# Expert loop of a mixture-of-experts kernel: ScalarE's copy of the next block's tokens moved ahead of its copy of a finished block's result

## The chip, the cores and the metric

One core of one Trainium2 chip. The metric is the device time of one execution in microseconds; the time before is 1798.47 us, the median of three runs (1798.45 to 1799.83).

## The reference, cut to what matters

The kernel computes one whole layer: a bidirectional mLSTM and Fourier mixer, then a mixture of experts with 64 experts of which each of 1024 tokens takes 8, plus a shared expert. The change touches only the routed experts. Tokens are sorted by expert and padded to blocks of 128 rows, and each block goes through one expert:

```python
def expert_block(args):
    xblk, e = args
    g, u = jnp.split(xblk @ w_expert_gu[e], 2, axis=-1)
    return (jax.nn.silu(g) * u) @ w_expert_down[e]
yb = lax.map(expert_block, (xb, block_e)).reshape(n_rows, d)
routed = jax.ops.segment_sum(yb * row_w[:, None].astype(yb.dtype), row_tok, num_segments=n_tok)
```

The gather is `xb = t[row_tok]`, and the `segment_sum` is a scatter-add of each block's 128 rows of 1024 floats into the rows of their tokens. With the inputs given there are 104 blocks.

## The kernel before, in words

Everything is float32. A matmul operand is split into a high part (rounded to fp32r) and a low part (the remainder), and each product is made of three matmuls: high by high, high by low, low by high. ScalarE (ACT) makes high parts with a copy, VectorE (DVE) makes low parts with a subtraction.

The expert loop works in steps, one for each block b, software-pipelined. Each engine has its own written-out order for a step (the function `step` in each engine's block), and semaphores join them. Two steps, for the two buffer parities p, make one turn of a hardware loop.

**TensorE (PE), step b.** `h_transposes(b-1)` (2 transposes, L1351, which wait for DVE's `h_rows(b-1)`), `x_transposes(b+1)` (8 transposes, L1330, into PSUM banks 0 and 1), `gate_up(b)` (24 matmuls, L1343 to L1345), `down(b-1)` (12 matmuls, L1365 to L1367, into PSUM banks 5 and 6). `gate_up(b)` waits for `m_xb` (both halves of block b's tokens), `down(b-1)` for `m_y` (banks 5 and 6 were read out by `y_evac(b-2)`).

**ScalarE, step b.** `h_high(b-1)` copies the transposed hidden rows; `y_evac(b-2, p)` copies the finished result of block b-2 from PSUM to the buffer yB[p]; `x_high(b+1)` copies the transposed tokens of block b+1 and is the high half; then `w_high` makes the high parts of weight chunks of 1024 columns (an expert has six, four of gate/up and two of down); then `silu(b)` (L911); then two more chunks. Which chunks are due is decided at run time from a table: a step in which the expert before last brings in its down weights and the next step's expert is a new one has four chunks ahead of `silu`, and two after it. Other steps have two chunks or none. All the copies have one line in the profile, L692, since they go through one helper; they are told apart by their tiles (`arena<-psum 128x1024` is `y_evac`, `split_rows<-psum 128x1024` is `x_high`, `split_rows<-psum 128x256` is `h_high`, `split_weights<-raw_weights` is `w_high`).

**VectorE, step b.** `h_low(b-1)` (L1931), `x_low(b+1)` (L1923 and L1927, waits for `x_high`), `w_low` for the same two or four chunks (L1938, one subtraction for each; every one of them waits for its own high part with `hi_split`), `h_rows(b)` (L1945, for which PE waits at the start of the next step), then `w_low` for two more chunks. The wait in `w_low` stands ahead of the addresses that it works out from registers:

```python
for c in chunks:
    dve.wait_ge(S("hi_split"), 6 * e + (c + 1))
    high = cols(wsplit, (1 - par) * (2 * WE) + 1024 * c, 1024).bitcast(F32)
    tt(cols(wsplit, ...), cols(raw, (1 - par) * WE + 1024 * c, 1024), high, ALU.subtract)
```

**GpSimd (POOL).** For block b, in step b+2: it waits for `m_xb` of block b+3, copies an index column (L642), issues the gather of block b+5 (L645), copies another index column (L652), then `add_rows(b)` waits for `m_y` (yB is filled) and for the scatter of block b-1 to have landed, and issues the scatter-add of block b (L656). Scatters are so done one after the other, since two of them may add to one row.

**SyncE (SP).** It loads the raw weights of an expert (2 MB gate/up, 1 MB down) into one of two buffers as `w_low` frees them (`lo_split`), and passes on their arrival to ScalarE by `gu_ready` and `dn_ready` (L518).

`y_evac(b-2, p)` waits for two things: that `down(b-2)` is done, and that the scatter of block b-4, which reads the same buffer yB[p], has landed:

```python
def y_evac(b, p):
    act.wait_ge(S("block_done"), b + 2)
    act.wait_ge(S(f"added{p}"), 8 * (b - p) + 16)
    copy(yB[:, p], psY).then_inc(S("m_y"), 1)
```

Of the kernel before, what the change touches and what calls it, by code (L numbers as in the profile page):

```python
# [105 lines left out]
def build(nc, a, out):  # L106

    ctx = ExitStack()
    with ctx:
# [62 lines left out]
        def bank(i):  # L172
            return psum[:, 512 * i:512 * i + 512]
# [516 lines left out]
        def _(act):  # L690
            def copy(o, i):
                return act.activation(o, i, ACT.Copy)  # L692
# [151 lines left out]
            def w_high(par, chunks):  # L844

                for c in chunks:
                    copy(cols(wsplit, (1 - par) * (2 * WE) + 1024 * c, 1024), cols(raw, (1 - par) * WE + 1024 * c, 1024)).then_inc(S("hi_split"), 1)
# [44 lines left out]
            def x_high(b, p):  # L892

                act.wait_ge(S("m_xt"), b + 1)
                if isinstance(b, int) and b == 1:
                    copy(xTh[p], psY).then_inc(S("m_xh"), 1)
                else:
                    copy(xTh[p], psum[:, 0:1024]).then_inc(S("m_xh"), 1)

            def h_high(b):  # L900
                act.wait_ge(S("m_ht"), b + 1)
                copy(hTh, bank(7)[:, 0:2 * P]).then_inc(S("m_hh"), 1)
# [6 lines that stand above are left out]
            def silu(b, p):  # L909
                act.wait_ge(S("m_gu"), b + 1)  # L910
                act.activation(sg[:, p], bank(3 + p)[:, 0:DE], ACT.Silu).then_inc(S("m_sg"), 1)  # L911
# [8 lines left out]
            def step(b, p, here, following):  # L920

                h_high(b - 1)
                if here is not None:
                    y_evac(b - 2, p)
                x_high(b + 1, 1 - p)
                if here is None:
                    act.wait_ge(S("dn_ready"), 2)
                    w_high(1, range(4, 6))
                else:
                    with act.If_ne(act.to_reg(here[0]), 0):  # L930
                        act.wait_ge(S("dn_ready"), here[1] + 2)
                        act.sem_inc(S("passed"), 1)
                        w_high(1 - (here[1] & 1), range(4, 6))
                first, par1 = following[0], 1 - (following[1] & 1)
                with act.If_ne(act.to_reg(first), 0):
                    act.wait_ge(S("gu_ready"), following[1] + 2)
                    act.sem_inc(S("passed"), 1)
                    w_high(par1, range(2))
                silu(b, p)
                with act.If_ne(act.to_reg(first), 0):  # L940
                    w_high(par1, range(2, 4))

            def word(b):
                return word_of(act, b)

            step(1, 1, None, fields(word(1)))
            act.wait_ge(S("table_ready"), 2)
            for i in range(2):
                act.wait_ge(S(f"acc_out{i}"), 64)
            rest = act.value_load(pairs_rest[0:1, 0:1], min_val=NE // 2 - 1, max_val=MAXB // 2 - 1)  # L950
            with act.Fori(0, rest) as i:
                one, two, three = pair_of(act, i)[0:3]
                step(2 * i + 2, 0, one, two)
                step(2 * i + 3, 1, two, three)
# [1115 lines left out]
```

## Time and profile before

| | us |
|---|---|
| median of three runs | 1798.47 |
| the profiled execution's own time | 1800.7 |
| its span, first to last instruction | 1798.9 |
| PE busy | 1711.2 (95%) |
| VectorE busy | 1146.1 (64%) |
| ScalarE busy | 797.5 (44%) |
| GpSimd busy | 522.0 (29%) |

The profile is one execution seen by the hardware profiler. In a timeline each row is the start of an instruction (or of several alike), how long they took, engine, line, operation and tiles, and in brackets how long the engine was idle just before and what ended the wait. All times are counted from the start of the span. PE is TensorE's matmul side, PEld its weight-load side; the first waits of a step are seen on both. "<-" in a list of waits names what was waited for, then total us, number of waits and the longest.

### The profile page before, as it was taken

To read this page: it belongs to the slowest core of one execution; us is meant where nothing else is said; L and a number is where in the kernel's file an instruction comes from. 1 tells how busy PE (TensorE), PEld (TensorE's weight loads), DVE (VectorE), ACT (ScalarE), POOL (GpSimd) and SP (SyncE) were. 2 spreads that over 40 slices of the span, in tenths; PEclk is the share of its full clock that TensorE was granted. 3 is DMA by queue.
4 is the path that set the end of the run, shared out by engine and by line. 5 is a ranking of instruction groups with operands and counts; after the bars stand their busy time and mean duration, and the time that the engine had idled before them with its cause. 6 is when DMAs were issued, how large, how long until landed. Compare 5 with 4: busy or idle time off the path is not lost.

```text
span 1798.9 us, 32529 instructions
## 1 busy us (share of the span) xinstructions
PE 1711.2 (95%) x7475; PEld 1237.0 (69%) x7476; DVE 1146.1 (64%) x1704; ACT 797.5 (44%) x1094; POOL 522.0 (29%) x569
## 2 busy tenths in 40 slices
PE   6999999998889999899999998999999999999987
PEld 1545454446854477788888777888888887888864
DVE  4783765403877869667538888653767687266646
ACT  0211112122231032466547787553767676265624
POOL 2000000004832320134334344433443343333321
PEclk9999999999999999999999999999999999999999
DMA  9652000011344241768859899866789789588863
GB/s 379 258 231 95 1 0 0 1 37 40 108 148 175 105 164 54 300 201 311 282 108 367 286 343 338 290 172 202 255 289 344 203 297 371 98 286 235 232 209 142
DMA packets 95503, 357.79 MB, mean 199 GB/s; under 512 B 19389, under 2 KB 19550, under 8 KB 86757
## 3 DMA queue, kind: packets, MB, share of 16 engines
q1 hardware_dynamic: 65298, 288.49, 42.0%
q0 software_dynamic: 30160, 68.76, 17.1%
q8 instruction: 23, 0.38, 0.1%
q14 instruction: 18, 0.15, 0.0%
q10 hardware_dynamic: 4, 0.02, 0.0%
HBM read 330.96 MB, written 70.62 MB: 223 GB/s over the span
## 4 chain that ended last, share of the span: by engine, by line
PE 72%; DMA 12%; DVE 6%; issue 3%; ACT 3%; SPq 1%; ACTq 1%; DVEq 1%; POOL 1%; POOLq 0%
PE psum L1343 8%; PE psum L1345 8%; PE psum L1344 8%; PE psum L1069 7%; DMA sum_rows<-arena,idxs 7%; PE psum L1174 5%; PE psum L1078 4%; PE psum L1330 4%; DMA raw_weights<-in_w_gu 4%; PE psum L1367 3%; PE psum L1365 3%; PE psum L1366 3%; PE psum L1016 3%; PE psum L1109 3%; ACT split_weights L692 2%
## 5 line engine op out<-in xcount | busy, mean ns | idle before, releaser
L1938 DVE TENSOR_TENSOR split_weights<-raw_weights,split_weights (+1 forms) x366 | 428.5, 1220 | 46.3 <-ACT split_weights L692 39.1
L692 ACT ACTIVATE split_weights<-raw_weights (+1 forms) x366 | 363.8, 1060 | 35.2 <-issue 23.6
L1343 PE MATMUL psum<-split_weights,split_rows 128*128 (+1 forms) x832 | 335.7, 403 | 2.5 <-DVE split_rows L1927 2.5
L1345 PE MATMUL psum<-split_weights,split_rows 128*128 (+1 forms) x832 | 326.3, 392 | 0.0
L1344 PE MATMUL psum<-split_weights,split_rows 128*128 (+1 forms) x832 | 325.1, 391 | 0.0
L692 ACT ACTIVATE arena<-psum 128x1024 f32<-128x1024 f32 (+6 forms) x187 | 154.5, 831 | 374.6 <-PE psum L1069 107.1
L656 POOL DMA_INDIRECT sum_rows<-arena,idxs x102 | 171.9, 1685 | 231.9 <-DMA sum_rows<-arena,idxs 189.5
L692 ACT ACTIVATE split_rows<-psum 128x256 fp32r<-128x256 f32 (+1 forms) x209 | 148.1, 709 | 136.8 <-PE psum L1351 134.0
L1345 PEld LDWEIGHTS psum<-split_weights,split_rows 128*128 128x128 f32 x832 | 156.9, 189 | 34.8
L1343 PEld LDWEIGHTS psum<-split_weights,split_rows 128*128 128x128 f32 x832 | 157.5, 189 | 31.8 <-DVE split_rows L1927 2.6
L642 POOL COPY idxg<-idxT 128x1 uint32 (+1 forms) x107 | 73.0, 682 | 366.5 <-DVE split_rows L1927 294.6
L1344 PEld LDWEIGHTS psum<-split_weights,split_rows 128*128 128x128 f32 x832 | 157.4, 189 | 30.1
L1365 PE MATMUL psum<-split_weights,split_rows 128*128 x416 | 161.9, 389 | 1.5 <-DVE split_rows L1931 1.5
L1367 PE MATMUL psum<-split_weights,split_rows 128*128 x416 | 162.5, 391 | 0.0
L1366 PE MATMUL psum<-split_weights,split_rows 128*128 x416 | 161.8, 389 | 0.0
L645 POOL DMA_INDIRECT arena<-t_rows,idxg x107 | 123.3, 1152 | 93.7 <-POOL idxg L642 91.5
L1927 DVE TENSOR_TENSOR split_rows<-psum,split_rows 128x1024 fp32r<-128x1024 f32 x104 | 126.3, 1214 | 0.0
L1069 PE MATMUL psum<-arena 128*128 128x512 f32 (+1 forms) x320 | 123.9, 550 | 1.3 <-DVE arena L1543 1.3
L911 ACT ACTIVATE arena<-psum 128x256 f32<-128x256 f32 x104 | 39.8, 383 | 186.8 <-PE psum L1345 186.8
L1931 DVE TENSOR_TENSOR split_rows<-psum,split_rows 128x256 fp32r<-128x256 f32 x104 | 43.7, 420 | 108.7 <-ACT split_rows L692 106.9
L1174 PE MATMUL psum<-arena 128*128 128x512 f32 x256 | 111.1, 592 | 0.8 <-issue 0.8
L1330 PE MATMUL psum<-cst,arena 128*128 128x128 f32 x840 | 111.5, 276 | 0.3 <-ACT arena L692 0.3
(306 smaller groups left out, 2300.6 us busy)
## 6 DMA issues: line engine op xcount, KB each, us to landing
raw_weights<-in_w_gu SPq DMA_DIRECT2D x62, 2048.0 KB, 11.5
raw_weights<-in_w_dn SPq DMA_DIRECT2D x62, 1024.0 KB, 10.3
arena<-in_w_ada SPq DMA_DIRECT2D x12, 2048.0 KB, 8.6
arena<-in_toks SPq DMA_DIRECT2D x18, 512.0 KB, 9.4
arena<-job_rows SPq DMA_DIRECT2D x16, 512.0 KB, 3.8
arena<-in_w_vog SPq DMA_DIRECT2D x1, 4160.0 KB, 14.5
arena<-in_w_qk SPq DMA_DIRECT2D x1, 4096.0 KB, 17.3
arena<-in_w_out SPq DMA_DIRECT2D x2, 2048.0 KB, 9.4
```

Source lines behind the costliest of these rows:

```text
L656: pool.indirect_dma_start(out=y_dram[:, :], out_offset=bass.IndirectOffsetOnAxis(ap=idxs[:, p:p + 1], axis=0), in_=yB[:, p], in_offset=Non ...
L692: return act.activation(o, i, ACT.Copy)
L1069: ins = mm(bank(q % 4)[:, 0:n], wqk[:, k, P * c:P * c + P], uT[:, k, o:o + n], start=(k == 0), stop=(k == 7))
L1174: ins = mm(o, mixT[:, k, P * j:P * j + P], wout[:, k, 512 * h:512 * h + 512], start=(k == 4), stop=(k == 3))
L1330: ins = pe.transpose(bank(5 + k // 4 if isinstance(b, int) and b == 1 else k // 4)[:, P * (k % 4):P * (k % 4) + P], xg[:, p, 0:D][:, k::8] ...
L1343: mm(bank(3 + p), xk, part(par, 0, 512 * k), start=(k == 0), stop=False)
L1344: mm(bank(3 + p), xk, part(par, 1, 512 * k), start=False, stop=False)
L1345: ins = mm(bank(3 + p), xl, part(par, 0, 512 * k), start=False, stop=(k == 7))
L1365: mm(bank(first + h), hk, part(par, 0, o), start=(k == 0), stop=False)
L1366: mm(bank(first + h), hk, part(par, 1, o), start=False, stop=False)
L1367: ins = mm(bank(first + h), hl, part(par, 0, o), start=False, stop=(k == 1))
L1938: tt(cols(wsplit, (1 - par) * (2 * WE) + (WE + 1024 * c), 1024), cols(raw, (1 - par) * WE + 1024 * c, 1024), high, ALU.subtract).then_inc( ...
```

## The change

In ScalarE's step, `x_high(b+1)` is put ahead of `y_evac(b-2)`. Nothing else is changed: the same instructions with the same waits.

```diff
             def step(b, p, here, following):
 
                 h_high(b - 1)
+                x_high(b + 1, 1 - p)
                 if here is not None:
                     y_evac(b - 2, p)
-                x_high(b + 1, 1 - p)
                 if here is None:
                     act.wait_ge(S("dn_ready"), 2)
                     w_high(1, range(4, 6))
```

## Rows read from the trace of the kernel before

**Rows 1.** Windows: us, busy time (count) by engine, PEclk, DMA share, GB/s

```profile
956.00:1123.50 167.50, 155.05 (x745) 127.39 (x744) 137.83 (x157) 129.13 (x156) 66.85 (x65) 0.99 0.93 330
...
1530.00:1740.00 210.00, 210.00 (x1032) 176.76 (x1030) 103.96 (x137) 104.75 (x137) 79.10 (x91) 1.00 0.72 208
```

**Rows 2.** Waits in the expert loop, 745 to 1740 us

```profile
POOL sum_rows L656 <- DMA sum_rows<-arena,idxs: 189.5, 63, 6.0
...
PEld psum L1351 <- DVE arena L1945: 34.4, 43, 3.1
ACT arena L692 <- DMA sum_rows<-arena,idxs: 24.2, 19, 2.7
...
PE psum L1351 <- DVE arena L1945: 20.3, 19, 2.7
ACT split_weights L692 <- SPq L518: 9.7, 6, 2.2
```

**Rows 3.** Waits of PE in the stretch 956 to 1123.5 us

```profile
PE psum L1351 <- DVE arena L1945: 12.4, 10, 2.7
```

**Rows 4.** Timeline of ScalarE, a step with four chunks, scatter landed in time

```profile
957.28 1.02 ACT L692 ACTIVATE arena<-psum 128x1024 f32<-128x1024 f32 x1
958.18 1.03 ACT L692 ACTIVATE split_rows<-psum 128x1024 fp32r<-128x1024 f32 x1
959.09 3.91 ACT L692 ACTIVATE split_weights<-raw_weights  x4
```

**Rows 5.** Timeline of VectorE, the same step

```profile
959.59 1.22 DVE L1927 TENSOR_TENSOR split_rows<-psum,split_rows 128x1024 fp32r<-128x1024 f32 x1
960.80 4.63 DVE L1938 TENSOR_TENSOR split_weights<-raw_weights,split_weights  x4
```

**Rows 6.** Timeline of PE: transposes that begin that step and the next

```profile
956.48 0.48 PE L1351 MATMUL psum<-cst,arena 128*128 128x128 f32 x2
956.80 1.06 PE L1330 MATMUL psum<-cst,arena 128*128 128x128 f32 x8
...
965.92 0.47 PE L1351 MATMUL psum<-cst,arena 128*128 128x128 f32 x2
```

**Rows 7.** Timeline of the loop's first step, which has no result to copy

```profile
750.25 1.06 PE L1330 MATMUL psum<-cst,arena 128*128 128x128 f32 x8
...
751.34 1.03 ACT L692 ACTIVATE split_rows<-psum 128x1024 fp32r<-128x1024 f32 x1 [0.51 <-PE psum L1330]
```

**Rows 8.** Timeline of ScalarE where a chunk's weights came late

```profile
972.49 2.01 ACT L692 ACTIVATE split_weights<-raw_weights  x2 [1.95 <-SPq L518]
```

**Rows 9.** Timeline of VectorE, the low part of that chunk

```profile
974.17 1.23 DVE L1938 TENSOR_TENSOR split_weights<-raw_weights,split_weights  x1 [1.58 <-ACT split_weights L692]
```

**Rows 10.** Timeline of VectorE, a step whose low parts began late

```profile
1458.69 4.63 DVE L1938 TENSOR_TENSOR split_weights<-raw_weights,split_weights  x4
```

**Rows 11.** Timeline of PE: transposes that begin that step and the next

```profile
1453.92 0.39 PE L1351 MATMUL psum<-cst,arena 128*128 128x128 f32 x2
...
1463.77 0.51 PE L1351 MATMUL psum<-cst,arena 128*128 128x128 f32 x2 [0.36 <-DVE arena L1945]
```

**Rows 12.** Timeline of a step whose scatter landed late, and the next transposes

```profile
1114.12 1.03 ACT L692 ACTIVATE arena<-psum 128x1024 f32<-128x1024 f32 x1 [2.70 <-DMA sum_rows<-arena,idxs]
...
1117.66 4.63 DVE L1938 TENSOR_TENSOR split_weights<-raw_weights,split_weights  x4
...
1122.74 0.51 PE L1351 MATMUL psum<-cst,arena 128*128 128x128 f32 x2 [2.67 <-DVE arena L1945]
```

**Rows 13.** Timeline of POOL: the index copy ahead of a gather, two steps

```profile
801.77 0.18 POOL L642 COPY idxg<-idxT 128x1 uint32 x1 [3.58 <-DVE split_rows L1927]
...
960.97 1.10 POOL L642 COPY idxg<-idxT 128x1 uint32 x1 [3.49 <-DVE split_rows L1927]
```

**Rows 14.** Chain that ended last: one of twelve scatters in a row

```profile
1060.37 10.43 DMA sum_rows<-arena,idxs
```

**Rows 15.** Windows around the one fall of TensorE's clock in the busy stretch

```profile
1017.70:1022.20 4.50, 4.50 (x19) 3.69 (x18) 3.40 (x6) 3.93 (x5) 1.60 (x1) 0.62 0.98 372
```

## The prediction, made before the changed kernel ran

> **What bounds the kernel now.** I read the windows of the expert loop first. PE is busy for all of the last 210, but for only 155.05 of 167.5 us between 956 and 1123.5, where the DMA share is 0.93 and the experts change nearly every block [rows 1]. So the loop runs at PE's pace, a little under the 9.44 us from transposes to transposes in [rows 6], except in stretches. The list of waits says what PE waits for: only the two transposes that begin a step, and always for VectorE's `h_rows`; 43 times on the weight-load side (34.4 us), 19 times long enough to be seen on the matmul side (20.3 us) [rows 2]. Those 43 are the steps with four weight chunks ahead of `h_rows`; in 43 - 19 = 24 of them everything is on time and PE only just waits. The 19 others have a cause further back: ScalarE held up in `y_evac` by a scatter that had not landed (19 waits, 24.2 us in all [rows 2]), or in `w_high` by weights (6 waits, 9.7 us [rows 2]). 12.4 of PE's 20.3 us lie in the dense stretch [rows 2, 3].
>
> **What the change removes.** In a late step the copy of the result waited 2.70 us, ran at 1114.12, and all behind it moved: the low parts began at 1117.66, 3.54 us after the start of `y_evac`, and PE idled 2.67 us [rows 12]. Now `x_high` and `x_low` are done by the time the scatter lands. What stays behind the wait is `w_high` and, behind that, the low parts. From the start of `y_evac` the path becomes: one copy, with the next starting 0.90 us later (957.28 to 958.18 [rows 4]), then the first chunk, then its low part. For the last link see below: 1.68 us from the start of a high chunk to the start of the low one. So 2.58 us instead of 3.54: a late four-chunk step is 0.95 us less late.
>
> This is not 0.95 for each. In the dense stretch the chain that ended last is one scatter after another, 10.43 us for one alone [rows 14], without the start of the next, against a step of 9.4; GpSimd waited for the previous scatter 63 times [rows 2]. The landings are paced by the scatters, and PE follows at a fixed distance. Shortening the distance moves PE forward once: **-0.95 us** for the dense stretch. The few late steps elsewhere have two chunks or none and cost PE nothing now.
>
> **What it moves.** `x_high` ran at 958.18, after `y_evac`. It needs the x transposes, which ran from 956.80; in the first step, where there is no result to copy, they began at 750.25 and `x_high` at 751.34, 1.09 us later [rows 7]. So in the step of [rows 4 to 6] `x_high` would begin at 957.89 and `y_evac`, 0.92 behind it, at 958.8, and end at 959.8. `down(b-1)` needs it only after the 24 gate matmuls, which end about two thirds into the step: no cost. `x_low` comes 0.3 us earlier (958.18 against 957.89): no gain by itself, since `gate_up(b+1)` is a step away.
>
> **What it adds.** `w_high` still comes third, but the idle time that ScalarE had after `h_high`, in which `y_evac` was hidden, is now spent waiting for PE's transposes. The first chunk starts not at 959.09 [rows 4] but at about 959.7, 0.6 us later. Now VectorE: today its first low part starts at 960.80, just as `x_low` ends [rows 5], and 1.71 us after the high chunk began. How much of this is slack? Where the weights themselves were late, ScalarE began the chunk at 972.49 and the low part began at 974.17 with VectorE idle for 1.58 us: 1.68 us from start to start [rows 8, 9]. Two copies take 2.01 us and four 3.91 [rows 4, 8], so one takes 1.06, and some 0.6 us pass between the end of the high part and the low part, with the engine idle: the wait stands ahead of the address arithmetic. Today this is hidden behind `x_low`, and there is no slack left (1.71 against 1.68). So the low parts start at 959.7 + 1.68 = 961.4 instead of 960.80, **0.6 us later**, in each four-chunk step.
>
> Is `h_rows` moved by as much? The four low parts run back to back for 4.63 us, the high parts come every 0.96 us (3.91 for four), so only the first matters; `h_rows` follows their end (960.80 + 4.63 = 965.43), and PE's next transposes start 0.49 behind it, at 965.92 [rows 4 to 6]. The trace has a natural experiment: a step in which the low parts began late by an overrun of the step before, 4.77 us after the transposes (1453.92 to 1458.69) where the on-time step has 4.32 (956.48 to 960.80). It took 9.85 us to the next transposes and PE waited 0.36; the on-time step took 9.44 [rows 5, 6, 10, 11]. The 0.45 us came through as 0.41. So an on-time four-chunk step pays 0.55 to 0.6 us; I take 0.6, since the chain is serial. The lower bound of this term is nothing (were the first low part after all to wait only for `x_low`), the upper the full 0.92 us of a copy.
>
> How many pay? Of the 24, some stand just ahead of a step whose weights arrive late (six such waits, 9.7 us [rows 2], several in consecutive steps; I take four steps ahead of them); the load runs on meanwhile, so the pay is taken off the next wait. Two more, by my reading of the steps, lie inside the scatter-paced stretch. 24 - 6 = 18 pay: 18 x 0.6 = **+10.8 us**. Steps with two chunks or none have 1.5 us or more to spare behind the low parts and pay nothing; if the cover were gone they would pay the same 0.6.
>
> **GpSimd and SyncE.** The index copy that starts the gather took 0.18 us in a step where VectorE was idle and 1.10 us in [rows 13]'s second, where the low parts had begun. In the new order `x_low` ends 0.3 us earlier and VectorE is then idle for nearly 1 us, so the copy will run in the gap; gather and scatter are issued up to 1.2 us earlier (0.92 + 0.3). Only where scatters pace the loop is this worth anything, once, at the entry to the dense stretch: between 0 and 1.2, I take **-0.9 us**, three quarters of it. The Trainium skill ("SBUF — State Buffer", Who interferes with whom) says that a VectorE instruction with two SBUF inputs blocks a GpSimd one that reads SBUF for its whole duration; by that rule the hold-up would be one full subtraction and the sum 0.3 us smaller. The copy was held for 0.92 us, not for the 1.2 of a subtraction, and the sum goes by the row. No SP or POOL instruction is passed by the moved one; SP's down load is released by low parts 0.6 us later, against loads used more than a step later: 0.
>
> **Sum.** 10.8 - 0.95 - 0.9 = +9 us. On the profiled execution that is a span of 1798.9 + 9 = 1807.9 and a time of 1800.7 + 9 = 1809.7; this execution stands 2.2 us above the median of the runs, so for the median I forecast 1798.5 + 9 = **1807.5 us**.
>
> **Rivals.**
> - *Rather faster.* The late steps are relieved and the on-time ones pay nothing, because the low part's address work is done before its wait or ScalarE's first chunk is not pushed back. Against it: [rows 8, 9], and that ScalarE cannot begin `x_high` before the transposes end. If then every late step in the dense stretch gave its wait back, the gain would be as much as the 12.4 us of [rows 3]: 1788 us as an end, with 1792 in the middle. It decides if the landing of scatters moves forward with PE, that is if a scatter in this stretch takes less than a step. Chance 0.07.
> - *No difference.* No pay in on-time steps, but landings stay where they are: -0.95 - 0.9, at most -3: 1796.5 us. Or the pay is absorbed by DMA in most steps (in the stretches with share 0.93 the transfers set the pace, and time given to them is not lost): +3. Chance 0.13.
> - *Worse than forecast.* All 24 pay and nothing is absorbed: +14.4. To this comes TensorE's clock: it fell once in the dense stretch, to 0.62 granted over 4.5 us (partly at 1.2 instead of 2.4 GHz) [rows 15]. It cost 0.38 x 4.5 = 1.7 us. More steps with idle time can bring one more fall: 1798.5 + 14.4 + 1.7 = 1814.6 us. The Trainium skill ("TensorE: Matmul & The Clock Gate", Part 1) says that the clock is gated by how busy the array has been lately. By that rule the new idle time counts towards a fall; the trace has one fall in a stretch with ten waits of PE [rows 3, 15], so few of them bring one. Chance 0.12.
>
> **How the numbers follow.** The forecast has 0.68. What a measurement of this kernel can tell from no change is 0.2%, 3.6 us. Slower: 0.68 + 0.12 = 0.80; same 0.13; faster 0.07. The range leaves out the faster case, the gaining part of the no-difference case and the tail of the worst: 1801 to 1813.5. It holds 0.3 to 0.8 us of pay in 18 steps, less the gains (18 x 0.3 - 1.85 = +3.5; 18 x 0.8 - 0.95 = +13.5), and a little at the low end.
>
> **What would show it.** Right: PE's transposes wait for `h_rows` still 43 times or so, but some 35 to 43 of them on the matmul side too, with the total up by 8 to 10 us; VectorE waits for `split_weights` in about 40 more steps, 0.9 us each; on-time four-chunk steps last 10.0 instead of 9.44 us; `y_evac` starts 0.9 after `x_high`; the index copy takes 0.2 us in nearly all steps; late steps begin their low parts 2.6 us after `y_evac` starts. Wrong: low parts that still follow `x_low` without a gap, or late steps that vanish altogether instead of moving.

## The result and the profile after

The changed kernel takes 1809.43 us, the median of four runs (1807.71 to 1811.19), against 1799.06 us for the kernel before in runs beside it: 10.4 us slower, a ratio of 1.0057 with a 95% interval of 1.004 to 1.0075. The forecast was 1807.5 us, 9 us above the 1798.47 of its time before. The profiled execution took 1810.08 us, its span is 1808.2 us, 9.3 us over the 1798.9 of the one before.

The waits of the expert loop after the change, from 745 to 1740 us, answer to [rows 2]:

```profile
POOL sum_rows L656 <- DMA sum_rows<-arena,idxs: 190.2, 62, 6.9
...
DVE split_weights L1938 <- ACT split_weights L692: 89.0, 84, 1.7
...
PEld psum L1351 <- DVE arena L1945: 43.7, 44, 1.9
...
PE psum L1351 <- DVE arena L1945: 25.2, 44, 1.4
...
ACT arena L692 <- DMA sum_rows<-arena,idxs: 5.9, 8, 1.9
ACT split_weights L692 <- SPq L518: 2.5, 3, 0.9
```

Two things are to be seen. The wait that was to be relieved is relieved: ScalarE waits for a landing 8 times and 5.9 us in all, where it was 19 times and 24.2 us (in the dense stretch 2.3 us where it was 12.5), and the longest wait of PE is 1.4 us where it was 2.7 [rows 2]. And the price is paid in every four-chunk step: PE's matmul side now idles in 44 steps where it was 19 (one of each is the loop's first step; the others are four-chunk steps, of which there are 43), and the weight-load side waits 43.7 us where it was 34.4. That these 9.3 us are just what the span has grown by is partly chance: some of the growth lies outside the loop, as shown below. VectorE waits 84 times, 89.0 us, for a high part of a weight chunk, where it was 34 times and 38.3 us.

One on-time four-chunk step shows how. ScalarE, then VectorE, then PE, from timelines of the changed kernel; they answer to [rows 4 to 6]:

```profile
961.98 1.03 ACT L692 ACTIVATE split_rows<-psum 128x1024 fp32r<-128x1024 f32 x1 [0.51 <-PE psum L1330]
962.90 1.02 ACT L692 ACTIVATE arena<-psum 128x1024 f32<-128x1024 f32 x1
963.80 3.90 ACT L692 ACTIVATE split_weights<-raw_weights  x4
```
```profile
963.37 1.22 DVE L1927 TENSOR_TENSOR split_rows<-psum,split_rows 128x1024 fp32r<-128x1024 f32 x1
965.51 4.63 DVE L1938 TENSOR_TENSOR split_weights<-raw_weights,split_weights  x4 [0.92 <-ACT split_weights L692]
```
```profile
960.54 0.51 PE L1351 MATMUL psum<-cst,arena 128*128 128x128 f32 x2 [0.48 <-DVE arena L1945]
...
970.59 0.51 PE L1351 MATMUL psum<-cst,arena 128*128 128x128 f32 x2 [0.46 <-DVE arena L1945]
```

ScalarE is idle for 0.51 us until the transposes are done, `y_evac` comes 0.92 us behind `x_high`, and the first weight chunk 3.26 us after the step's transposes, where it was 2.61 (959.09 - 956.48). The low part starts 1.71 us after the high one, as before, but now VectorE stands idle for 0.92 of them. The step lasts 10.05 us instead of 9.44.

A late four-chunk step of the changed kernel, ScalarE, VectorE and PE, answers to [rows 12]:

```profile
1115.65 1.03 ACT L692 ACTIVATE arena<-psum 128x1024 f32<-128x1024 f32 x1 [0.37 <-DMA sum_rows<-arena,idxs]
1116.57 2.00 ACT L692 ACTIVATE split_weights<-raw_weights  x2
```
```profile
1118.27 2.36 DVE L1938 TENSOR_TENSOR split_weights<-raw_weights,split_weights  x2 [1.41 <-issue]
```
```profile
1112.81 0.50 PE L1351 MATMUL psum<-cst,arena 128*128 128x128 f32 x2 [1.06 <-DVE arena L1945]
...
1123.84 0.50 PE L1351 MATMUL psum<-cst,arena 128*128 128x128 f32 x2 [1.45 <-DVE arena L1945]
```

The low part starts 2.62 us after `y_evac` does, where it was 3.54. PE waits 1.45 us instead of 2.67. The starts of PE's transposes also give the balance along the way. The changed kernel was 4.67 us behind after the first step of the dense stretch (970.59 against 965.92 [rows 6]), but only 1.10 behind at its end (1123.84 against 1122.74 [rows 12]): the stretch gave back 3.6 us on balance, though two of these steps became longer by 0.6 us each. It was 8.51 us behind when the loop ended (1748.24 against 1739.73, both from the timelines of PE). The rest is the tail, whose granted clock was 0.85 over 60 us where it was 0.90.

The windows of the dense stretch, before at [rows 1], say that TensorE's clock did not fall there this time:

```profile
956.00:1123.50 167.50, 157.10 (x754) 128.21 (x753) 140.56 (x159) 133.15 (x159) 63.15 (x66) 1.00 0.94 334
```

### The profile page after: what moved, and what is told of

It reads as the page before. It is cut to its first block, busy times and chain, and to the rows that moved or that the text cites. A ratio compares the mean times of both kernels' runs of the same rounds, so it can differ in the third digit from the quotient of the medians.

```text
span 1808.2 us, 32529 instructions
## 1 busy us (share of the span) xinstructions
PE 1715.7 (95%) x7475; PEld 1236.4 (68%) x7476; DVE 1146.0 (63%) x1704; ACT 803.0 (44%) x1094; POOL 512.9 (28%) x569
## 4 chain that ended last, share of the span: by engine, by line
PE 64%; DMA 9%; DVE 8%; ACT 7%; issue 6%; ACTq 2%; DVEq 2%; SPq 1%; POOL 1%; POOLq 0%
PE psum L1069 7%; DMA sum_rows<-arena,idxs 6%; PE psum L1343 6%; PE psum L1345 6%; PE psum L1344 6%; ACT split_weights L692 5%; PE psum L1174 5%; PE psum L1330 4%; PE psum L1078 4%; PE psum L1016 3%; PE psum L1109 3%; PE psum L1367 2%; PE psum L1365 2%; PE psum L1366 2%; DVE split_weights L1938 2%
## 5 line engine op out<-in xcount | busy, mean ns | idle before, releaser
L645 POOL DMA_INDIRECT arena<-t_rows,idxg x107 | 163.9, 1532 | 93.7 <-POOL idxg L642 91.4
L642 POOL COPY idxg<-idxT 128x1 uint32 (+1 forms) x107 | 26.5, 248 | 376.3 <-DVE split_rows L1927 304.2
L1945 DVE SCALAR_TENSOR_TENSOR arena<-psum,gcol,arena 128x256 f32<-128x256 f32 x104 | 50.0, 481 | 95.3 <-ACT arena L911 92.7
```

## The experiments

**h_static: the changed kernel with constant addresses on VectorE.** The subtraction is written once for each buffer parity, so that no address is worked out behind the wait.

```diff
-                for c in chunks:
-                    dve.wait_ge(S("hi_split"), 6 * e + (c + 1))
-                    ...
+                def run(q):
+                    for c in chunks:
+                        dve.wait_ge(S("hi_split"), 6 * e + (c + 1))
+                        ...
+                with dve.If_ne(dve.to_reg(par), 0):
+                    run(1)
+                with dve.If_ne(dve.to_reg(par), 1):
+                    run(0)
```

> The changed kernel, with VectorE's weight subtraction written once for each buffer parity inside a branch, so that its addresses are constants and nothing stands between its wait and the subtraction. Theory (the 0.6 us of address arithmetic behind the wait, uncovered by the new order, is what an on-time four-chunk step pays): the low part follows the high part by under 0.1 us instead of 0.6, on-time four-chunk steps go back from 10.05 to about 9.43 us, PE's waits on the matmul side fall from 44 to under 20, and the time is 1793 to 1798 us, below both kernels. Rival (ScalarE's later start itself is the cost, address work or not, or VectorE and GpSimd collide): steps stay near 10 us and the time near 1809.

Measured: 1793.83 us (ten runs), against 1799.42 for the kernel before: ratio 0.9974 (0.9965 to 0.9983). Against the changed kernel's 1809.43 this is 15.6 us less, for the same order and the same work. The on-time step, ScalarE, VectorE and PE:

```profile
817.39 3.90 ACT L692 ACTIVATE split_weights<-raw_weights  x4
```
```profile
818.49 4.70 DVE L1939 TENSOR_TENSOR split_weights<-raw_weights,split_weights 128x1024 fp32r<-128x1024 f32 x4 [0.21 <-ACT split_weights L692]
```
```profile
814.14 0.50 PE L1351 MATMUL psum<-cst,arena 128*128 128x128 f32 x2
...
823.64 0.51 PE L1351 MATMUL psum<-cst,arena 128*128 128x128 f32 x2
```

From start of the high part to start of the low part it is 1.10 us instead of 1.71: the 0.6 us between the two engines are gone, VectorE idles 0.21 instead of 0.92, and the step lasts 9.50 us. On-time four-chunk steps of this kernel last 9.3 to 9.7 us, 9.47 on average, so a tenth of a microsecond is still paid. ScalarE starts its chunks exactly as late as in the changed kernel (3.25 us into the step against 3.26), so its lateness alone costs little. The matmul side waits for `h_rows` 16 times, 12.3 us.

**b_static: the same constant addresses in the kernel before.** The diff is that of h_static on the old order.

> The kernel before with the same constant addresses. Theory: in the old order the arithmetic is hidden behind x_low in every on-time step, so only the steps in which weights arrive late gain, 0.6 us in each of five or six: 1795.5 to 1799 us, and on-time four-chunk steps stay at 9.43. Rival (the arithmetic costs in both orders): all 43 steps shorter, 1790 or less. Second rival (the added branches cost more than they save): above 1801.

Measured: 1797.95 us, ratio 0.9995 (0.9986 to 1.0005), so no difference that can be told. The theory's range holds it; the saving in late-weight steps is not resolved. In the old order the address work is hidden: on-time four-chunk steps last 9.30 to 9.44 us, as before. With constant addresses in both, the new order is then 4.1 us faster than the old one (1793.83 against 1797.95), and that is clear of the noise.

**b_twice: one more copy ahead of `y_evac`, old order.**

```diff
             def y_evac(b, p):
                 ...
+                copy(slack[:, 0:512], psY[:, 0:512])
                 copy(yB[:, p], psY).then_inc(S("m_y"), 1)
```

> The kernel before with one more ScalarE copy (128x512, to a scratch buffer) ahead of y_evac in every step: ScalarE's chunks come about 0.5 us later, with no change of order and none to VectorE or GpSimd. Theory: every on-time four-chunk step pays those 0.5 us in full and the others nothing: 18 x 0.5 to 24 x 0.5, so +9 to +12: 1808 to 1811 us. Rival (the price is not set by when the chunks start): within 2 us of 1799.

Measured: 1808.48 us against 1799.42: ratio 1.0053 (1.0038 to 1.0068), +9.1 us. The extra copy moved what followed by 0.48 us (950.07 to 950.55), and the weight chunks with it:

```profile
950.07 0.59 ACT L693 ACTIVATE slack<-psum 128x512 f32<-128x512 f32 x1
950.55 1.03 ACT L693 ACTIVATE arena<-psum 128x1024 f32<-128x1024 f32 x1
951.46 1.04 ACT L693 ACTIVATE split_rows<-psum 128x1024 fp32r<-128x1024 f32 x1
952.36 3.92 ACT L693 ACTIVATE split_weights<-raw_weights  x4
```
```profile
PE psum L1353 <- DVE arena L1947: 25.2, 45, 2.2
```

With no change of order, 45 waits of PE instead of 19 and 25.2 us, the same total as in the changed kernel. On-time four-chunk steps last 9.79 to 9.93 us here, where they were 9.34 to 9.44. So half a microsecond of delay ahead of VectorE's four low parts is enough to cost this kernel about 9 us. The extra copy puts off the result's copy too, and with it the issue of the scatter, so this run alone doesn't say that all of the 9 us are the low parts'.

**a_pool_slow: the changed kernel with slower GpSimd steps.**

```diff
                     pool.wait_ge(S("m_xb"), 2 * i + (p + 4))
+                    pool.tensor_copy(slacki[:, 0:1], idxT[:, bass.ds(2 * i + (p + 5), 1)])
+                    for q in range(5):
+                        pool.memset(slack[:, 8 * q:8 * q + 8], 0.0)
                     gather(bass.ds(2 * i + (p + 5), 1), 1 - p, 4 * i + (2 * p + 6))
```

> The changed kernel with six small GpSimd instructions (one index copy, five memsets of 8 columns) ahead of each gather, so that gather and scatter are issued about 1 us later, as before the change. Theory: that matters only where scatters pace the loop, once at its entry: 0 to +1.5 us on 1809.4. Rival (the earlier scatters are what emptied the late waits of the dense stretch): +3 us or more, and ScalarE's waits for landings back from 8 to 15 or more.

Measured: 1810.59 us (1809.0 to 1811.24), ratio 1.0064 (1.0049 to 1.0078) to the kernel before; the interval overlaps with that of the changed kernel, so the 1.2 us between them are not resolved. The groups of GpSimd's added instructions in this kernel (count, then total busy time and mean ns):

```profile
L677 POOL MEMSET slack<- 128x8 f32 x505 | 29.0, 143 | 0.0
L675 POOL COPY slacki<-idxT 128x1 uint32 x101 | 23.0, 228 | 274.9 <-DVE split_rows L1932 274.9
```

They were busy for 52 us in 101 steps, about 0.5 us a step, but the scatter was not put off. The gather and the index copy behind it (which the scatter needs), in the changed kernel and then in this one, in a step that begins at 960.54 and 960.55 us:

```profile
965.80 1.86 POOL L645 DMA_INDIRECT arena<-t_rows,idxg  x1 [0.85 <-POOL idxg L642]
967.66 0.25 POOL L652 COPY idxs<-idxT 128x1 uint32 x1
```
```profile
966.11 1.57 POOL L647 DMA_INDIRECT arena<-t_rows,idxg  x1 [0.85 <-POOL idxg L644]
967.68 0.24 POOL L654 COPY idxs<-idxT 128x1 uint32 x1
```

The gather's issue starts 0.31 us later and takes 0.29 us less, so what stands behind it starts at the same point of the step. ScalarE's waits for landings, 7 times and 6.2 us, could therefore not come back by this run, and it does not decide between the theory and its rival. The traces before and after say more. In the dense stretch GpSimd stood waiting for the scatter before to land ahead of 16 of its 17 scatters in the old order (63.7 us) and of 15 of 16 in the new one (74.7 us), so inside the stretch an earlier gather could not bring a scatter forward. That leaves ScalarE's new order as the likely cause of the relief there; what an earlier scatter is worth at the entry to the stretch was not tested.

**n_before and n_after: both orders without the scatter-adds.** The indirect scatter is replaced by a transfer of one row to a spare one, so these kernels leave out the routed experts' sums.

```diff
-                pool.indirect_dma_start(out=y_dram[:, :], ..., compute_op=ALU.add).then_inc(S(f"added{p}"), 16)
+                pool.dma_start(spare[p:p + 1, :], cst[0:1, 0:D]).then_inc(S(f"added{p}"), 16)
```

> The kernel before with the routed scatter-adds left out (a 4 KB transfer takes the place of each, so the routed experts' sums are missing from the output). Theory: no wait for a landing is left, DMA is lighter, and what stays above 9.35 us a step are the 0.08 us of on-time four-chunk steps and perhaps some late weights: 1779 to 1788 us.

> The changed kernel with the same scatter-adds left out. Theory: without late landings only the price of the new order is left, 0.62 us in each of 43 four-chunk steps, little of it absorbed: 22 to 27 us above the same kernel in the old order. Rival (the price is tied to the scatters or to GpSimd): under 12 us above it.

Measured: 1779.56 and 1805.68 us, 26.1 us apart. PE's transposes, of two steps of the loop 101 steps apart, in the old order and in the new:

```profile
758.71 0.39 PE L1350 MATMUL psum<-cst,arena 128*128 128x128 f32 x2
...
1706.53 0.39 PE L1350 MATMUL psum<-cst,arena 128*128 128x128 f32 x2
```
```profile
760.64 0.39 PE L1350 MATMUL psum<-cst,arena 128*128 128x128 f32 x2
...
1734.72 0.39 PE L1350 MATMUL psum<-cst,arena 128*128 128x128 f32 x2
```

That is 947.82 us and 974.08 us, 26.3 more, or 0.61 us for each of the 43 four-chunk steps. The waits say the same: the matmul side waits for `h_rows` once in the old order and 44 times, 20.6 us, in the new. So 26 us is the price of the order by itself. In the real kernel it costs 10.4, so steps that scatters and weights make late anyway take in the other 16. Turned round: scatters and the DMA load that they bring cost the kernel before some 20 us (1800.23 beside 1779.56), and the changed kernel only about 4.

**d_order: `y_evac` one place later still.**

```diff
                 x_high(b + 1, 1 - p)
-                if here is not None:
-                    y_evac(b - 2, p)
                 ...
                         w_high(1 - (here[1] & 1), range(4, 6))
+                if here is not None:
+                    y_evac(b - 2, p)
                 first, par1 = following[0], 1 - (following[1] & 1)
```

> The changed kernel with y_evac one place later still, between the two chunks of down weights and the two of gate/up. Theory: the first low part starts when x_low ends (3.55 us into the step), so the four low parts are two and two, with the second pair waiting for a high part that ends 5.75 us into the step and for 0.6 us of addresses: h_rows about 0.25 us later than in the kernel before, on-time steps 9.7 us. Late landings hardly matter. 1796 to 1803 us. Rival (any later y_evac costs PE at down): steps over 9.9 us, 1806 or more.

Measured: 1799.25 us against 1800.23, ratio 0.9994 (0.9983 to 1.0005): the same as the kernel before, 10 us better than the changed one. In the timeline of VectorE of this kernel the four low parts are two and two:

```profile
960.55 2.36 DVE L1938 TENSOR_TENSOR split_weights<-raw_weights,split_weights  x2
963.33 2.36 DVE L1938 TENSOR_TENSOR split_weights<-raw_weights,split_weights  x2 [0.42 <-issue]
```

The first pair starts as `x_low` ends, the second waits 0.42 us, and on-time four-chunk steps last 9.52 to 9.66 us. ScalarE waits for landings 3 times, 3.5 us.

**d_static: d_order with constant addresses** (the diff is that of h_static).

> The same order with constant addresses on VectorE. Theory: both pairs of low parts are back to back, on-time four-chunk steps 9.35 to 9.43 us, late landings and late weights are mostly absorbed: 1787 to 1794 us, the fastest of all. Rival (y_evac that late holds up down, or the branches cost): 1797 or more.

Measured: 1793.78 us (1790.91 to 1795.56) against 1800.23, ratio 0.9966 (0.9954 to 0.9977). It beats both kernels, but not h_static (1793.83), which it was expected to beat. The low parts run back to back, and an on-time four-chunk step lasts 9.31 to 9.44 us, about what steps with two chunks or none do (9.35):

```profile
959.03 4.66 DVE L1939 TENSOR_TENSOR split_weights<-raw_weights,split_weights 128x1024 fp32r<-128x1024 f32 x4
```

What this saves in on-time steps is lost in late ones. From the list of the waits of this kernel:

```profile
POOL sum_rows L656 <- DMA sum_rows<-arena,idxs: 224.3, 59, 7.7
...
ACT arena L692 <- DMA sum_rows<-arena,idxs: 15.6, 11, 3.8
...
ACT split_weights L692 <- SPq L518: 12.9, 11, 1.8
...
PE psum L1365 <- ACT arena L692: 2.9, 3, 1.3
```

ScalarE waits 15.6 us for landings where h_static has 6.8, and 12.9 us for weights where h_static has 15.7. The last row is `down` waiting for `y_evac`, 3 times; the only other kernel that has this wait is d_order, once for 0.8 us, and both have `y_evac` in the later place. GpSimd's waits for landings have gone up from 189.5 [rows 2] to 224.3 us. I read this as PE running ahead until the landing of a scatter stops it; that was not tested by itself.

## Why the prediction was right

The direction and the mechanism were right, and the size within 1.4 us (10.4 against 9.0). That the size came so close is in part luck, since several terms were off and made up for each other. By the steps of the prediction:

- **The pay of an on-time four-chunk step, 0.6 us.** Right: 10.05 against 9.44 us in the example, 26.3 / 43 = 0.61 with nothing to hide it (n_before, n_after), 0.48 us of delay bringing +9.1 us (b_twice).
- **Its cause: no slack, since 0.6 us of address work stands behind VectorE's wait.** Right, and shown: without it the same order takes 15.6 us less (h_static), and in the old order it is hidden (b_static).
- **How many pay, 18, and what is absorbed.** Mis-sized on both sides. By the starts of PE's transposes in the two traces, all 24 on-time steps became 0.45 to 0.67 us longer, 14.6 us in all, and not 18 with 10.8. Three of them lie in the dense stretch. The six steps whose weights came late gave back 3.9 us, and ScalarE's waits for weights fell from 9.7 to 2.5 us. The prediction had six steps that pay nothing in the end, 6 x 0.6 = 3.6 us: four ahead of late weights and two in the dense stretch.
- **The dense stretch, -0.95 and -0.9.** The sum of 1.85 was too small. Ten four-chunk steps of the stretch that had been late for other reasons than weights became 3.8 us shorter. The balance of 3.6 us over the stretch is made of this, of 1.0 us from one step with late weights (11.06 us before, 10.06 after), and of 1.2 us lost in two on-time steps. The distance from `y_evac` to the low part fell by 0.92 us, as forecast.
- **The term of -0.9 for GpSimd.** No run supports it. The gather did start 1.2 us earlier in the step (6.35 us after the transposes, now 5.15), but its issue then took 1.86 us instead of 1.17, so the scatter was issued only 0.52 us earlier (8.73, now 8.21). The clock's fall in this stretch before, priced at 1.7 us, did not recur, which may account for part of what came back beyond the -0.95. How the rest divides between landings and PE's pace was not settled.
- **The beginning and the tail.** Not forecast: some 0.8 us each, 1.6 of the 9.3 us of the span. The loop between them grew by 7.7 us and not by 9: 14.6 paid, 3.9 and 3.8 given back, and 0.8 in small differences of other steps. In the first step PE waited for a gather to land (1.8 us), and the tail ran at a lower clock. Neither needs the new order: the trace of b_static, in the old order, has the same wait (1.7 us, in a first step of 12.89 us) and the same granted clock of 0.85 in its tail, and that of h_static, in the new order, has neither (first step 9.47 us, 0.90 in the tail). They vary between executions.
- **The index copy in [rows 13].** The prediction took its hold-up of 0.92 us as less than one subtraction of 1.2. But the copy began 0.17 us after the subtraction did (960.97 against 960.80 [rows 5]), so the row fits a hold-up to the end of that subtraction as well. It changed nothing in the sum.
- **What to look for.** I had expected PE's waits to grow by 8 to 10 us on the matmul side. They grew by 4.9 there (20.3 to 25.2) and by 9.3 on the weight-load side, which also sees the short waits. VectorE's waits for high parts came as expected, 50 more and 51 us more.
- **The rivals.** "Rather faster" fell with the order as it is, but h_static shows what it would take: once the pay is gone, the kernel is 5.6 us faster than the one before, 4.1 of them by the order (beside b_static). "All 24 pay and nothing is absorbed" was half true: all 24 paid, and late steps gave back some 7 us. The fall of the clock by more idle steps did not come: four-chunk steps with 0.4 to 1.5 us of idle time each left the granted clock at 1.00 over the dense stretch. The loop's one fall was in its first step, to 0.73 from 750 to 755 us, after PE had waited for 1.08 and 1.82 us with only 0.5 us of work between.

## What to carry to other kernels

Before moving an operation ahead of a wait, ask which idle time hides what is overtaken: here `y_evac` filled, free of charge, the time in which ScalarE waits for PE, and the change spent that time on waiting. A step that feeds the next engine through a wait has to be counted to the instruction behind that wait, address arithmetic included; with constant addresses the same order was 0.3% faster than the kernel before instead of 0.6% slower. Late steps and on-time steps pulled against each other here, so count both kinds, and count what late steps give back of a price paid just before them. And when an experiment is meant to delay something, look in its trace for whether the thing was delayed.

## What the runs showed of the hardware that was not expected

In VectorE's weight subtraction, working out three addresses from registers between the semaphore wait and the subtraction cost 0.6 us while VectorE was idle (1.71 us from high part to low part against 1.10 without), and nothing that could be told when an earlier instruction of VectorE was still running (b_static).

GpSimd's copy of one index column took 692 ns on average in the loop before and 243 after, with no edit to GpSimd. In the timelines it takes 0.18 us where VectorE is idle, as it now mostly is at that point, and 1.0 to 1.1 us beside VectorE's subtractions. The gather that follows took 1155 ns before and 1550 after. So most of what the copy gained, the gather's issue gave back. With VectorE's subtractions at the same place, the gather's issue ended at the same time whether it started at 965.80 or at 966.11 us (after, a_pool_slow): a GpSimd instruction that is issued earlier beside them need not be done earlier.
